# Row-half scores and whole-operand products in banded attention, late normalization in forgetting attention, adaLN columns ahead of its first scores

## What is computed

```python
def swa_prompt(q, k, v, sinks):      # group A: 8 query heads, 2 key heads, width 64
    ...                              # a row reads its chunk of 64 and the 2 chunks before
    s = jnp.einsum('bcqhgd,bckhd->bchgqk', qc, kb) * SCALE
    m = jnp.maximum(jnp.max(s, -1, keepdims=True), sink)
    p = jnp.exp(s - m)
    p = p / (jnp.sum(p, -1, keepdims=True) + jnp.exp(sink - m))
    o = jnp.einsum('bchgqk,bckhd->bcqhgd', p, vb)

def fox_prompt(q, k, v, logf):       # group B: 8 heads, causal, forgetting
    F = jnp.cumsum(logf, axis=1)
    ...                              # blocks of 128 query rows
    s = jnp.einsum('bqhd,bkhd->bhqk', qi, k) * SCALE + Fi[..., None] - Fk[:, :, None, :]
    p = jax.nn.softmax(jnp.where(kpos <= qpos, s, -jnp.inf), axis=-1)
    o = jnp.einsum('bhqk,bkhd->bqhd', p, v)
```

## Time and profile before

| | us |
|---|---|
| median of 3 runs (3151.2 to 3164.45) | 3152.11 |
| the profiled execution | 3151.35 |
| its span, first to last instruction | 3149.6 |

### The profile page before, as it was taken

How to read it: one execution, slowest core, us unless ns; L and a number is a source line. 1 busy time by engine, 2 the same in 40 slices (tenths; PEclk the granted TensorE clock), 3 DMA queues, 4 the chain that set the end, 5 groups by cost and what they waited for, 6 DMA issues and landing times.

```text
span 3149.6 us, 45412 instructions
## 1 busy us (share of the span) xinstructions
PE 2880.0 (91%) x18607; PEld 2609.5 (83%) x18607; DVE 1272.4 (40%) x2289; ACT 921.8 (29%) x1751; POOL 253.2 (8%) x149
## 2 busy tenths in 40 slices
PE   5999888899799999999969989788979999999997
PEld 3999566568699999999859976654859999999996
DVE  3113756512733333333450247563155333333335
ACT  4122545513311122211231236463242211112222
POOL 0000007600000000000000000373000000000000
PEclk7999789969899999999979989798889999999998
DMA  7110331221111111111341114211311111111112
GB/s 268 55 55 30 123 104 28 60 87 60 59 45 49 40 53 40 44 50 40 123 156 53 44 56 142 67 29 50 108 70 41 50 43 40 53 40 50 43 55 83
DMA packets 158369, 211.49 MB, mean 67 GB/s; under 512 B 8864, under 2 KB 131792, under 8 KB 157712
## 3 DMA queue, kind: packets, MB, share of 16 engines
q1 hardware_dynamic: 158240, 209.66, 20.3%
HBM read 170.45 MB, written 31.00 MB: 64 GB/s over the span
## 4 chain that ended last, share of the span: by engine, by line
PE 81%; DVE 7%; POOL 5%; ACT 3%; issue 2%; DMA 2%; SPq 0%; ACTq 0%; DVEq 0%; POOLq 0%
PE ps L1375 23%; PE ps L1377 22%; PE ps L1376 22%; POOL pbuf L530 5%; PE ps L1649 1%; DVE th L994 1%; PE ps L1552 1%; PE ps L1428 1%; PE ps L1561 1%; PE ps L1631 1%; DVE xr L1016 1%; PE ps L1551 1%; DMA raw<-w_in 1%; PE ps L1406 1%; PE ps L1612 1%
## 5 line engine op out<-in xcount | busy, mean ns | idle before, releaser
L1375 PE MATMUL ps<-hh,wh 128*128 128x352 f32 x2304 | 756.5, 328 | 37.7 <-DVE hl L1002 36.3
L1377 PE MATMUL ps<-hh,wl 128*128 128x352 f32 x2304 | 747.7, 325 | 0.0
L1376 PE MATMUL ps<-hl,wh 128*128 128x352 f32 x2304 | 746.4, 324 | 0.0
L1375 PE MATMUL ps<-uh,wh 128*128 128x352 f32 x1536 | 499.5, 325 | 1.5 <-ACT r_t L924 1.5
L1376 PE MATMUL ps<-ul,wh 128*128 128x352 f32 x1536 | 493.0, 321 | 0.0
L1377 PE MATMUL ps<-uh,wl 128*128 128x352 f32 x1536 | 492.7, 321 | 0.0
L1375 PEld LDWEIGHTS ps<-hh,wh 128*128 128x128 f32 x2304 | 438.5, 190 | 43.4 <-issue 26.7
L1376 PEld LDWEIGHTS ps<-hl,wh 128*128 128x128 f32 x2304 | 440.1, 191 | 0.4
L1377 PEld LDWEIGHTS ps<-hh,wl 128*128 128x128 f32 x2304 | 438.5, 190 | 0.0
L1353 DVE TENSOR_TENSOR y<-ps,y 128x352 f32<-128x352 f32 x384 | 198.1, 523 | 426.0 <-PE ps L1377 425.8
L976 DVE TENSOR_TENSOR wl<-raw,wh 128x2048 fp32r<-128x2048 f32 (+1 forms) x90 | 206.2, 2291 | 382.0 <-ACT wh L539 382.0
(11 more groups left out here) (233 smaller groups left out, 3419.9 us busy)
## 6 DMA issues: line engine op xcount, KB each, us to landing
ada_v<-w_ada SPq DMA_DIRECT2D x32, 1024.0 KB, 5.1
raw<-w_up SPq DMA_DIRECT2D x32, 1024.0 KB, 5.5
raw<-w_down SPq DMA_DIRECT2D x32, 1024.0 KB, 4.9
x_kept<-xr SPq DMA_DIRECT2D x12, 1408.0 KB, 9.0
ada_w<-w_ada SPq DMA_DIRECT2D x16, 1024.0 KB, 9.2
raw<-w_in SPq DMA_DIRECT2D x16, 1024.0 KB, 4.9
xf<-x_kept SPq DMA_DIRECT2D x2, 4224.0 KB, 12.7
xr<-x_kept SPq DMA_DIRECT2D x2, 4224.0 KB, 14.1
```

The lines of the kernel that those rows point to most:

```text
L1375: pe.matmul(out, w_hi, m_hi, start=start and k == 0, stop=False)
L1376: pe.matmul(out, w_hi, m_lo, start=False, stop=False)
L1377: return pe.matmul(out, w_lo, m_hi, start=False, stop=stop and k == nk - 1)
```

## The change

1. **Banded scores in row halves.** Queries and keys keep high and low parts in separate tiles, with both head halves on the two halves of the partitions. All matmuls of a turn take 64 rows, alternating between the halves, each half into its own bank: 2 mask matmuls (a small selector `wsel` by two rows of `winb` kept on each 32 partitions) and 12 others in place of 8 and 8.
2. **Banded products whole.** The transposed probabilities are copied out once (`pt_out`, DVE) in fp32 and multiplied with `vs` itself, 64 output rows at a time: 4 fp32 matmuls in place of 12. `pt_hi`, `pt_lo`, `v_hi`, `v_lo` go.
3. **Banded normalization on POOL**, as a `tensor_tensor` with the 4 reciprocals of a row broadcast; DVE keeps `denominators`. `spbuf` has 4 buffers, transposes and products come one turn later.
4. **Splits moved.** `k_hi`, `k_lo` go into the last unit of the projection; `q_hi`, `q_lo` handle 256 rows of a key head, 8 times in a layer.
5. **Forgetting attention normalized late.** `expo` writes row sums to `fsum`; `denominators` takes 8 reciprocals at once, twice per `t`; PE spreads them over 64 partitions with 8 small fp32 matmuls a time (two more groups in `FG`), ACT copies them to `th`, DVE multiplies the finished output half (`o_norm`) into `th`, and `o_hi`, `o_lo` read `th`. POOL has nothing to do there, and transposes wait for the exponentials.
6. **`mod_columns` ahead** of the first two scores of the forgetting attention.

```diff
             for l in range(DEPTH):
-                pool.memset(svh[:, :, 64:128].bitcast(F32), 0.0).then_inc(sm("sz_ok"), 1)
-                pool.memset(svl[:, :, 64:128].bitcast(F32), 0.0).then_inc(sm("sz_ok"), 1)
+                for w in range(16):
+                    W = P if w % 8 == 0 else 256
+                    pv = spbuf[w % 4][:, 0:4 * W].rearrange("p (h n) -> p h n", h=4)
+                    pool.wait_ge(sm("s_rd"), l * 16 + w + 1)
+                    pool.tensor_tensor(pv, pv, st[:, w % 4, 16:20][:, :, None].broadcast_to([P, 4, W]), ALU.mult).then_inc(sm("s_norm"), 1)
...
-                for x in range(64):
-                    n = (FOX_ORDER[x % 8] + 1) * P
-                    pool.wait_ge(sm("fs_rd"), l * 64 + x + 1)
-                    pool.tensor_scalar(pbuf[x % 3][:, 0:n], pbuf[x % 3][:, 0:n], st[:, x % 4, 2:3], None, ALU.mult).then_inc(sm("fs_norm"), 1)
...
+                        if u == N_TM - 1 and 2 <= i < 6:
+                            k_hi((i - 2) // 2, i % 2)
...
+                def q_hi(ch):
+                    g, qc = ch // 4, slice(ch % 4 * 256, ch % 4 * 256 + 256)
+                    if ch == 4:
+                        act.wait_ge(sm("f_kept"), (l + 1) * 16)
+                    copy(sqh[g][:, :, qc], qs[:, 2 * g:2 * g + 2, qc], scale=SCALE).then_inc(sm("sq_hi"), 1)
...
+                def pt_out(w):
+                    nk = 1 if w % 8 == 0 else 2
+                    dve.wait_ge(sm("st_mm"), l * 16 + w + 1)
+                    if w >= 2:
+                        dve.wait_ge(sm("so_mm"), l * 16 + w - 1)
+                    dve.tensor_copy(spt[w % 2][:, 0:nk, :, :].rearrange("p k h n -> p k (h n)"), ps[:, 4:4 + nk, :]).then_inc(sm("st_out"), 1)
...
+                def denominators(t, b):
+                    dve.wait_ge(sm("fs_exp"), (l * 4 + t) * 16 + 12 + 4 * b)
+                    dve.reciprocal(fsum[:, t % 2, b, :], fsum[:, t % 2, b, :]).then_inc(sm("fs_rd"), 1)
+
+                def o_norm(t, b):
+                    g = FG.index((12 + 3 * b, -1, b))
+                    dve.wait_ge(sm("ft_act"), (l * 4 + t) * NFA + n_fa(g + 1))
+                    dve.wait_ge(sm("pv_mm"), (l * 4 + t) * 4 + (2, 4)[b])
+                    c0 = (512, 0)[b]
+                    dve.tensor_tensor(th[:, t + 4, c0:c0 + 512], ps[:, 6 + b, :], th[:, t + 4, c0:c0 + 512], ALU.mult).then_inc(sm("fo_norm"), 1)
...
-                        for h in range(2):
-                            pe.matmul(view[:, h, 0:W], identb, msk, start=(h == 0), stop=False, skip_group_check=True)
-                        for h in range(2):
-
-                            hd = 2 * h + bb
-                            r = slice(64 * bb, 64 * bb + 64)
-                            pe.matmul(view[:, h, 0:W], sq1[w % 2][:, hd, :], sk1[g][:, k0:k0 + W], start=False, stop=False, skip_group_check=True)
-                            ins = pe.matmul(view[:, h, 0:W], sq1[w % 2][r, hd, :], sk2[g][r, k0:k0 + W], start=False, stop=(h == 1), skip_group_check=True)
+                    for d in range(2):
+                        pe.matmul(view[d][:, :, 0:W], wsel[half[d], :], winb[half[d], None, 256 - W:256].broadcast_to([64, 2, W]),
+                                  start=True, stop=False, skip_group_check=True)
+                    for h in range(2):
+                        qh, ql = sqh[g][:, h, i * P:(i + 1) * P], sql[:, 2 * g + h, i * P:(i + 1) * P]
+                        for qp, kp in ((qh, sk1[g]), (qh, sk2[g]), (ql, sk1[g])):
+                            for d in range(2):
+                                ins = pe.matmul(view[d][:, h, 0:W], qp[half[d], :], kp[half[d], k0:k0 + W], start=False,
+                                                stop=(h == 1 and qp is ql), skip_group_check=True)
...
-                    todo = [(kb, d) for kb in range(len(kbs)) for d in range(2)]
-                    for x, (kb, d) in enumerate(todo):
-                        vsl = slice(64 * d, 64 * d + P)
-                        out = ps[:, 6 + w % 2, 0:256]
-                        ins = three(out, svh[:, kbs[kb], vsl], svl[:, kbs[kb], vsl],
-                                    spth[w % 2][:, kb, 2 * d:2 * d + 2, :], sptl[w % 2][:, kb, 2 * d:2 * d + 2, :], x, len(todo))
+                    for kb, kbl in enumerate(kbs):
+                        for d in range(2):
+                            ins = pe.matmul(ps[64 * d:64 * d + 64, 6 + w % 2, 0:256], vs[:, kbl, 64 * g:64 * g + 64],
+                                            spt[w % 2][:, kb, 2 * d:2 * d + 2, :], start=(kb == 0), stop=(kb == len(kbs) - 1), skip_group_check=True)
...
-                for w in range(-2, 17):
+                for w in range(-2, 18):
                     if 0 <= w + 2 < 16:
                         scores(w + 2)
-                    if 0 <= w < 16:
-                        p_transposes(w)
                     if 0 <= w - 1 < 16:
-                        products(w - 1)
+                        p_transposes(w - 1)
+                    if 0 <= w - 2 < 16:
+                        products(w - 2)
...
-                    pe.wait_ge(sm("fs_norm"), l * 64 + x + 1)
+                    pe.wait_ge(sm("fs_exp"), l * 64 + x + 1)
...
+                        if k0 == -1:
+                            pe.wait_ge(sm("fs_rd"), (l * 4 + t) * 2 + k1_ + 1)
+                            for i in range(4):
+                                j = FOX_ORDER.index(i if k1_ else 4 + i) % 4
+                                for h in range(2):
+                                    ins = pe.matmul(ps[64 * h:64 * h + 64, 4 + g % 2, i * P:(i + 1) * P],
+                                                    fsum[:, t % 2, k1_, 4 * h + j:4 * h + j + 1].broadcast_to([P, 64]), ident[:, :],
+                                                    start=True, stop=True, skip_group_check=True)
...
-                scores(0)
-                scores(1)
-
                 for b in range(16):
                     ins = mod_columns(ps[:, 7, 4 * b:4 * b + 4], mrow[b // 8][:, (b % 8) * 256:(b % 8 + 1) * 256])
                 ins.then_inc(sm("mod_mm"), 1)
+                scores(0)
+                scores(1)
```

More of the change, by code:

```diff
@@ L185, in build @@
         zerob = small("zerob", [P, P], BF16)
+        wsel = small("wsel", [P, P], BF16)
         vt = small("vt", [P, 80], F32)
@@ L208, in build @@
         epst = small("epst", [P, 1], F32)
+        fsum = small("fsum", [P, 2, 2, 8], F32)
         vrow = at("vrow", [80, P], F32, sz + 6400)
@@ L318, in build, with fg_end @@
         FG = [(e, 4 * bb, min(4 * bb + 4, FOX_ORDER[e % 8] + 1)) for e in range(16) for bb in range(NBT[e])]
-        FG_ACT = [k1_ - k0 == 4 and k0 == 0 for e, k0, k1_ in FG]
+        FG.insert(BT[13], (12, -1, 0))
+        FG.append((15, -1, 1))
+        NFG = len(FG)
+        FG_ACT = [k0 == -1 or k1_ - k0 == 4 and k0 == 0 for e, k0, k1_ in FG]
+        def fg_end(e):
+            return max(g + 1 for g in range(NFG) if FG[g][0] <= e)
         def n_fa(g):
@@ L709, in expo @@
                     act.wait_ge(sm("s_mn"), l * 16 + w + 1)
-                    if w >= 2:
-                        act.wait_ge(sm("st_mm"), l * 16 + w - 1)
+                    if w >= 4:
+                        act.wait_ge(sm("st_mm"), l * 16 + w - 3)
+                    elif w >= 2:
+                        for i in range(3):
+                            act.wait_ge(sm(f"ko_out{i}"), (l + 1) * 48)
                     else:
@@ L744, in _ @@
                         expo(w + 1)
-                    if 0 <= w < 16:
-                        pt_hi(w)
                     if 0 <= w - 2 < 16:
                         o_hi(w - 2)
-                    if 2 <= w + 3 < 16:
-                        q_hi(w + 3)
-                    if w == -1:
-                        v_hi(0)
-                    if w == 0:
-                        for i in range(3):
-                            act.wait_ge(sm(f"ko_out{i}"), (l + 1) * 48)
-                        k_hi(1)
-                    if w == 8:
-                        v_hi(1)
+                    if w >= 0 and w % 2 == 0 and w // 2 + 2 < 8:
+                        q_hi(w // 2 + 2)
                 act.wait_ge(sm("so_lo"), (l + 1) * 16)
@@ L797, in pt_out @@
                     for g, (e_, k0, k1_) in enumerate(FG):
-                        if e_ == e and FG_ACT[g]:
+                        if e_ == e and k0 == -1:
+                            act.wait_ge(sm("ft_mm"), pr * NFG + g + 1)
+                            copy(th[:, t + 4, 512 - 512 * k1_:1024 - 512 * k1_], ps[:, 4 + g % 2, :]).then_inc(sm("ft_act"), 1)
+                        elif e_ == e and FG_ACT[g]:
                             used = pt_used(t, h, i // 2)
@@ L808, in _ @@
                 expo(0)
-                for x in range(65):
+                for x in range(72):
                     t, e = x // 16, x % 16
@@ L816, in _ @@
                         o_hi(t - 1, 0)
-                    if e == 3 and t:
+                    if e == 5 and t:
                         o_hi(t - 1, 1)
```

(25 more changed lines are left out.)

159 lines of the change are left out of this document (51 added, 108 removed).

## The result

The changed kernel takes 3030.27 us (median of 4 runs, 3027.49 to 3032.43), the kernel before 3158.03 beside it: a ratio of 0.9603, 95% interval 0.9577 to 0.9628. The profiled execution took 3032.43 us, 118.9 less than that of before. In the rows PE is TensorE and PEld its weight loads, DVE is VectorE, ACT ScalarE, POOL GpSimd and SP SyncE.

The account below looks back on a forecast made before the run. The prediction took PE's work and the ring through the query split to bound banded turns, and PE's waits for POOL to slow the forgetting attention. Terms sum to -55.65 us a layer, -111.3 from 3151.35: 3040.0 us, range 3008 to 3100.

Parts of the forecast that it names:

- Start: Start of the banded attention: key splits move into the projection's last unit, so scores start earlier, -4.3 us a layer.
- Banded turn: Banded attention: PE's four pieces sum to 4.5 us, 4.7 with gaps, against 6.86 before; scores taken at 1.5.
- the lower of the three ends given: Scores of a banded turn: 1.0 us if matmuls run two at a time; other ends 1.9 and 4.2.
- POOL's multiply: Banded normalization: two-operand multiply of 1024 numbers taken as 3.5 us (ends 2.98 and 6.0), hidden under turns of 4.7.
- POOL's lock: Rival, banded turns: POOL's read holds off DVE, 2 us net a turn, turns of 6.0, 3071 us; chance 0.03.
- The whole banded stage: Banded attention of a layer, start to end: from 122.2 us to 81.4, -40.8.
- the 5 us for turns at the lower clock: Term of the banded stage's sum: two turns still at 1.2 GHz, 2.5 us more each.
- Entry: Entry of the forgetting attention: adaLN records start at POOL's last memset, beside the DMAs PE waited for; -4.1 us a layer.
- Forgetting attention: Forgetting attention without POOL: 16 of 19.6 us of PE's waiting go, row sums add 8.8; net -7.2 us a layer.
- Tail: End of the forgetting attention: the last half's multiply stands ahead of its splits, +0.75 us a layer.

Follow-up runs that it names:

- e1: Changed kernel with a banded turn's score matmuls of one row half all first, the other half's behind them, instead of alternating; 3038.47 us.
- e3: Changed kernel with POOL's two-tensor banded multiply replaced by four one-tensor multiplies of 256 columns, each with one number of a row; 3024.61 us.
- e7: Changed kernel with the 64 adaLN records behind the first two scores of the forgetting attention again; 3039.45 us.
- e5: Changed kernel with the forgetting attention normalized by POOL's multiplication as before, without row sums, `th` and `o_norm`; 3049.61 us.
- e4: Changed kernel with another order of DVE's banded instructions, so that POOL's multiply lies beside the maximum and the copy; 3028.62 us.
- e9: Changed kernel with POOL's banded multiply as four one-tensor multiplies, DVE's reciprocals ahead of its copy, adaLN records ahead of the wait for POOL's memsets; 3016.44 us.
- e10: Changed kernel with DVE's banded maximum and copy placed beside POOL's multiply, and adaLN records ahead of the wait for POOL's memsets; 3016.05 us.

## Why the forecast was right, and where its steps were not

The time lies 10 us under the forecast of 3040 and inside its range. That it came so near is in part luck, since several wrong terms cancel. By its steps:

- **Start**: this step is right, -3.9 against -4.3, with the splits hidden in the last unit of the projection, whose blocks keep their distance of 3.51 us.
- **Banded turn**: the mechanism is right, PE's term was too large. The scores take 1.03 us, not 1.5: two at a time, the lower of the three ends given; e1 shows 1.50 for the order that doesn't alternate. The other pieces measured 1.02, 1.00 and 1.02. PE's own turn is 4.04, and the eleven turns from 328.55 to 377.11 average 4.41 us instead of 4.7, with PE's waits for DVE in about every second one. Here the page that the forecast named (the Trainium skill, TensorEngine Tiling (Array Packing), Key Properties) was the better guide: by its parallel tiles the scores would be 1.0, and the trace agrees with 1.03.
- **POOL's multiply**: 1.90 us, not 3.5. The row taken as nearest was the one-tensor form, 2.98 us for 1024 numbers; the two-tensor form is the quicker one. It is hidden either way.
- **POOL's lock**: this rival, given 0.03, does happen, so the forecast's reading of the earlier trace rows fails as evidence: the row shows POOL's one-tensor form, the change brings the two-tensor form, and e3 shows that they differ. The rival's price was too large, because POOL runs 1.90 us instead of 3.5 and DVE's maximum covers 1.2 of it: some 3.5 us a layer by e3, not 16. The page behind the rival (the Trainium skill, SBUF — State Buffer, Who interferes with whom) is borne out by 0.16 becoming 0.85 beside the two-tensor multiply; for the one-tensor multiply, which DVE's instructions pass but for its first 0.3 us or so, the measurement differs from it, and decides.
- **The whole banded stage**: the sum came near (77.3 against 81.4) by terms that cancel. The first transposes came 7.35 us after the first mask, at 325.24 (9 forecast until the first full turn). The next twelve turns took 51.9 us, not 59.4: the turns were shorter, and the 5 us for turns at the lower clock did not come, since the clock was full before the first whole turn. The end, from 377.11 on, took 18.1 us, not 13: from the last transposes (386.65) on there are their own 1.0 us, the modulate and products of two turns (4.1, not 2.0) and 1.7 us of waiting for a load.
- **Entry**: this step is right, -4.0 against -4.1, by the mechanism named (e7).
- **Forgetting attention**: a sum that came out near (-9.6, -8.3 against -7.2) from terms that did not. Of 19.6 us of waiting, 16 were to go; PE's idle time fell by 9.9, because the exponentials came late more often, as the forecast had named but not priced. The row sums cost their 8.7 (8.8 forecast). What closed the gap is a term that the forecast didn't have: PE's other work took 8.3 us less in layer 0 and 6.7 in layer 1 (without the row sums), while the clock rose from 0.93 to 0.97 and 0.96; e5 ties both to this part of the change. That the sum came near is luck.
- **Tail**: this step is right, +0.8.

## What to carry to other kernels

Cost an instruction by a row of the same form, not of the same size: two tensors or one changed POOL's duration by a third and whether DVE could run beside it. Where two engines share a stage, put the instructions that read PSUM beside the other engine's multiply and the short ones with two SBUF operands outside it. Here that order restored their durations (e4), but by itself it did not change the time clearly. A wait taken from PE can pay twice, once by itself and once by the clock of the work behind it; so look at the granted clock of a stage with waits before pricing their removal.

## What was not expected of the hardware

- A POOL multiply of 128x1024 fp32 numbers by a broadcast second tensor takes 1.90 us, the one by a number of each row 2.98. Beside the first, DVE's two-operand SBUF instruction of four numbers took up to 1.05 us instead of 0.16; beside the second it took 0.16 in the median and at most 0.39 (e3).
- Matmuls over row halves into two banks run two at a time if they alternate (14 in 1.03 us) and in part if they don't (1.50).
- 64 small matmuls took 11.51 us when the clock was still at 2.4 GHz as they began (e9, behind 1.31 us of idle time) and 13.78 when it had fallen before (behind 5.06 us); in e10 they took 13.79 behind 1.31 us, so the idle time just ahead of them does not decide alone.
